# GLA and NSA attention in one block of 44 slots, with the eight sample items at every fourth slot from the tenth

## The reference, cut to what matters

```
x = LN1(a*x + 0.5*FFN1(x))
(gq, gk, gv, ga, gr, nq, kc, vc, ks, vs, kw, vw, ng) = split(x @ w_in)
log_a = log_sigmoid(ga @ w_gate2 + b) / 16
o_g, S = gla_chunked(gq, gk, gv, log_a, S0)            # 4 heads, dk 128, dv 256
o_g = head_rms_norm(o_g) * silu(gr)
q, kc, ks, kw = rope(...)                              # 16 query heads, 4 kv heads, hd 64
k_cmp, v_cmp = gelu(blocks(kc|vc) @ w1) @ w2           # 15 compressed rows per sequence
o_n = g0*cmp_attention + g1*sel_attention + g2*window_attention
x = LN2(a*x + [o_g | o_n] @ w_out)
x = LN3(a*x + 0.5*FFN2(x))
```

## Time and profile before

| | us |
|---|---|
| median of 3 runs | 2891.38 (2885.6 to 2896.63) |
| the profiled execution | 2894.41 |
| its span, first to last instruction | 2892.6 |
| TensorE busy | 2787.4 (96%) |
| DVE, ACT, POOL busy | 1579.8, 469.2, 789.0 |
| mean granted TensorE clock | 0.938 |

### The profile page before, as it was taken

The page is one execution under the profiler, slowest core; times in us unless marked ns, Lnnn a source line. Parts: engine busy times, 40 slices in busy tenths (PEclk is TensorE's granted clock), DMA queues, the critical chain, the costliest instruction groups (busy, mean ns, idle before and its releaser), DMA issues. The chain is left out here.

```text
span 2892.6 us, 45504 instructions
## 1 busy us (share of the span) xinstructions
PE 2787.4 (96%) x17763; PEld 2657.3 (92%) x17763; DVE 1579.8 (55%) x1547; ACT 469.2 (16%) x1098; POOL 789.0 (27%) x578
## 2 busy tenths in 40 slices
PE   8999999999999999999898998979999999999997
PEld 7999999899999889997686777969999999999996
DVE  5555555455555565543647435565565565555555
ACT  2110001111000220001424542041100000000002
POOL 1332332132234520000424002533213322322353
PEclk9999999999999999999656777979999999999998
DMA  6555555455555535663221214435465455555542
GB/s 185 153 150 156 149 145 155 123 153 149 156 150 144 133 104 151 145 148 106 92 88 32 59 38 116 116 102 145 135 169 146 132 158 159 142 140 161 153 130 82
DMA packets 735289, 379.76 MB, mean 131 GB/s; under 512 B 65515, under 2 KB 729963, under 8 KB 735163
## 3 DMA queue, kind: packets, MB, share of 16 engines
q1 hardware_dynamic: 735098, 378.93, 48.0%
q10 hardware_dynamic: 128, 0.05, 0.0%
HBM read 369.62 MB, written 13.38 MB: 132 GB/s over the span
## 5 line engine op out<-in xcount | busy, mean ns | idle before, releaser
L318 PE MATMUL bank<-xh_before,wh_before 128*128 128x320 f32 x2112 | 657.6, 311 | 13.8 <-DVE wl_before L336 13.7
L320 PE MATMUL bank<-xh_before,wl_before 128*128 128x320 f32 x2112 | 656.0, 311 | 0.0
L319 PE MATMUL bank<-xl_before,wh_before 128*128 128x320 f32 x2112 | 655.9, 311 | 0.0
L318 PE MATMUL bank<-xh_after,wh_after 128*128 128x320 f32 x1664 | 521.4, 313 | 22.0 <-DVE wl_after L336 13.4
L334 DVE CAST wh_before<-raw 128x2048 fp32r<-128x2048 f32 (+1 forms) x196 | 219.8, 1121 | 579.8 <-PE bank L320 537.3
L319 PE MATMUL bank<-xl_after,wh_after 128*128 128x320 f32 x1664 | 518.4, 312 | 0.0
L320 PE MATMUL bank<-xh_after,wl_after 128*128 128x320 f32 x1664 | 518.3, 311 | 0.0
L336 DVE TENSOR_TENSOR wl_before<-raw,wh_before 128x2048 fp32r<-128x2048 f32 (+1 forms) x196 | 463.3, 2364 | 6.7
L334 DVE CAST wh_after<-raw 128x2048 fp32r<-128x2048 f32 (+1 forms) x168 | 184.8, 1100 | 435.8 <-PE bank L320 435.6
L318 PEld LDWEIGHTS bank<-xh_before,wh_before 128*128 128x128 f32 x2112 | 399.5, 189 | 15.5 <-issue 12.1
L336 DVE TENSOR_TENSOR wl_after<-raw,wh_after 128x2048 fp32r<-128x2048 f32 (+1 forms) x168 | 409.4, 2437 | 5.8
(11 more groups left out here) (232 smaller groups left out, 3419.2 us busy)
## 6 DMA issues: line engine op xcount, KB each, us to landing
raw<-in_w_ffn_in SPq DMA_DIRECT2D x176, 1024.0 KB, 5.8
raw<-in_w_ffn_out SPq DMA_DIRECT2D x128, 704.0 KB, 4.8
raw<-in_w_in SPq DMA_DIRECT2D x36, 1024.0 KB, 5.6
raw<-in_w_in SPq DMA_DIRECT2D x16, 512.0 KB, 5.3
raw<-in_w_out SPq DMA_DIRECT2D x16, 512.0 KB, 4.3
raw<-in_w_out SPq DMA_DIRECT2D x64, 128.0 KB, 3.8
proj<-in_cache_cmp_kv SPq DMA_DIRECT2D x64, 64.0 KB, 2.4
raw<-in_state_gla SPq DMA_DIRECT2D x8, 512.0 KB, 4.6
```

Source lines behind the costliest of these rows:

```text
L318: pe.matmul(out, L.wh[a][:, w], hi[:, k], start=(k == 0), stop=False)
L319: pe.matmul(out, L.wh[a][:, w], lo[:, k], start=False, stop=False)
L320: last = pe.matmul(out, L.wl[a][:, w], hi[:, k], start=False, stop=(k == nk - 1))
```

## The change

`gla` and `attention` become one function with one block, `mixing_stage`. What it does:

- A start does what the first `gla` block and the start of `attention` did, in another order: six tiles (the keys) are rotated first, with DVE doing both of their products; then DVE makes the decay and the first two differences, and only then are the other eight tiles rotated. POOL makes the level-0 keys in the midst of its part of those eight. Token turns lie between the rotations, six of them after the compression. The compressed rows come last.
- Then 44 slots run. In slot i each engine does its part of attention as before, and after it `gla_step(i)`: step 0 the key turn and level 0, odd steps up to 15 a level, even steps up to 16 a sample's state, steps 17 to 20 two outputs each, step 21 the last state, steps 22 and 23 the mean squares, later steps the norm.
- GLA has two PSUM banks (6 and 7) in turn for all its products; attention keeps the others, so that the compressed scores have one bank instead of two, and turned keys and probabilities share one.
- Sample items stand at slots 9, 13, ... 37. Their keys are turned in halves over two slots. Their three small products with new and compressed rows become one, of 48 rows.
- The differences are made for half of each group with the right sign, so the absolute value on ACT is gone, and level keys and queries are scaled on one half of the columns.
- The causal mask is added in place to the last 128 columns of the scores only, and the maximum is read from PSUM.
- The space comes from the residual `xT`: it is stored to memory during the projection (2.62 MB) and loaded back at slot 24.

The diff, cut to what the prediction speaks of:

```diff
@@ projection, SyncE
                 segment(seg_a, 8, 0, 1)
+                sp.wait_ge(L.ln["kept"], before.t0 + KD)
+                sp.dma_start(L.x_kept, L.xT[:]).then_inc(L.x_out, 16)
                 segment(seg_r, 4, 8)
-def gla(L, s):
+def mixing_stage(L, s):
...
+    B, QL, KL, att = (L.xT[:, 4 * i:4 * i + 4] for i in range(4))
+    roped = [T_KV + i for i in (0, 1, 4, 5, 8, 9)] + [T_NQ + i for i in range(8)]
+    NR, NK = len(roped), 6
...
-    FIRST, EVERY = 17, 3
+    FIRST, EVERY = 9, 4
...
+    gjobs = [("turn", t) for t in range(3)] + [("score", 0, j) for j in range(3)]
+    for step in range(1, 2 * LEVELS + 1):
+        if step % 2:
+            gjobs += [("score", (step + 1) // 2, j) for j in range(parts((step + 1) // 2))]
+        else:
+            gjobs += [("inter", step // 2 - 1), ("state", step // 2 - 1, 0), ("state", step // 2 - 1, 1)]
+    O_STEP = 2 * LEVELS + 1
+    P_STEP, MS_STEP = O_STEP + 4, O_STEP + 5
...
+    def gbank(job):
+        return bank[6 + gjob_no[job] % 2]
@@ tensor
+            def claim(job):
+                j = gjob_no[job]
+                if j >= 2:
+                    pe.wait_ge(g_free[j % 2], j // 2)
+                return gbank(job), g_made[j % 2]
...
             def scores(i):
                 if i >= 2:
-                    pe.wait_ge(masked, 2 * (i - 1))
-                main, small = bank[i % 2], bank[2 + i % 2]
+                    pe.wait_ge(exped, 3 * (i - 1))
+                main, small = bank[i % 2], bank[2]
...
+                    if i:
+                        pe.wait_ge(masked, 2 * i)
                     pe.matmul(small[:, 32:48], qT, k_cmp[r, NB, p], start=True, stop=True).then_inc(scored, 1)
...
-                    for n in range(3):
-                        mm = pe.matmul(o, v_small[:, n, b, p * P:(p + 1) * P], pt[0:16, 4 + n, q],
-                                       start=False, stop=(n == 2))
+                    mm = pe.matmul(o, v_small[:, b, p * P:(p + 1) * P], pt[0:48, 4, at], start=False, stop=True)
...
+            for i in range(NR):
+                rotate(i)
+                if i >= 2:
+                    turn_tokens(i - 2)
+            pe.wait_ge(by_sin, NR)
+            for n in (1, 0):
+                compress(n)
+            for i in range(EARLY, NJ):
+                turn_tokens(i)
+            compressed_rows()
+            pe.wait_ge(biased, GH)
+            for i in range(SLOTS):
+                for n in range(2):
+                    if i + 2 - n in seq:
+                        turn_keys(seq[i + 2 - n], n)
                 if i < NI:
                     scores(i)
                 if LAG <= i < NI + LAG:
                     turn(i - LAG)
                 if i > LAG:
                     outputs(i - LAG - 1)
+                gla_step(i)
@@ vector
+            def gla_step(g):
+                if g < O_STEP and g % 2 == 0:
+                    lv = g // 2
+                    if lv + 2 <= LAST:
+                        difference(lv + 2)
+                    if lv < LAST:
+                        q_level(lv + 1)
+                    if g:
+                        state(lv - 1)
+                    else:
+                        merge(0)
+                elif g < O_STEP:
+                    merge((g + 1) // 2)
...
+            for i in range(NK, NR):
+                rope(i)
...
+            for i in range(SLOTS):
+                if i <= NI:
+                    item(i)
+                gla_step(i)
@@ gpsimd
+            for i in range(NK, NR):
+                pool.wait_ge(rope_done, i - 1)
+                pool.tensor_tensor(xc[:, i % 2], proj[:, roped[i]], L.cst[:, K_COS:K_COS + T], ALU.mult
+                                   ).then_inc(by_cos_pool, 1)
+                if i == NK + 3:
+                    k_level(0)
@@ scalar
+            for i in range(9):
+                take_tokens(i)
+            decay(0)
+            act.activation(EB[:], B[:, :, TP:T], ACT.Exp).then_inc(chain_a, 1)
+            decay(1)
+            for i in range(9, EARLY):
+                take_tokens(i)
...
+            act.activation(gr, gr, ACT.Silu).then_inc(acted, 1)
+            for i in range(EARLY, NJ):
+                take_tokens(i)
+            for i in range(SLOTS):
...
+                if LAG <= i < NI + LAG:
+                    take(i - LAG)
+                if i > LAG:
+                    out(i - LAG - 1)
                 if i < NI:
                     exps(i)
+                gla_step(i)
@@ sync
+                if i == MS_STEP + 2:
+                    for h in range(2, GH):
+                        await_made(sp, ("ms", h))
+                    sp.dma_start(L.xT[:], L.x_kept).then_inc(L.x_back, 16)
```

More of the change, by code:

```diff
@@ L186, in build @@
             L.cmp_w2 = sb("cmp_w2", [P, 2, HD], scope=mixing)
[L187 to L191, removed]
+            mixing_stage(L, mixing)
         open_operands(L, "after")
@@ L824, in settle @@
         self.eng.wait_ge(self.sem, self.n)
-def gla(L, s):
+def mixing_stage(L, s):
     nc, A, O, bank, proj = L.nc, L.A, L.O, L.bank, L.proj
     NS = NB * TS
[L832 to L845, removed]
+    ident = L.cst[:, K_ID:K_ID + P]
     q = proj[:, T_GQ:T_GQ + GH]
@@ L1271, in attention @@
-def attention(L, s):
-    nc, A, O, bank, proj = L.nc, L.A, L.O, L.bank, L.proj
-    mix = proj[:, T_NQ:T_NQ + 8]
-    ident = L.cst[:, K_ID:K_ID + P]
-    LAG = 3
+    inter = L.sb("inter", [P, 2 * GH, NS], scope=s)
+    s0 = [L.raw[i][:, 1024:2048].rearrange("p (h v) -> p h v", h=GH) for i in range(2)]
+    o_var, o_t = ([proj[:, at + h] for h in range(GH)] for at in (T_GQ, T_GK))
+    o_r = [proj[:, T_KV + 6 + 4 * (h // 2) + h % 2] for h in range(GH)]
+    LAG, NV = 3, 2
     RING = LAG + 1
-    S = [L.sb(f"scores{i}", [P, 2, GW], scope=s) for i in range(2)]
+    NEW, WIN, CMP = PAST, GW, 2 * GW
@@ new lines, in mixing_stage @@
+    g_made = [L.sem(f"gla_bank_made{i}") for i in range(2)]
+    g_free = [L.sem(f"gla_bank_free{i}") for i in range(2)]
+    state_in = [L.sem(f"state_in{i}") for i in range(2)]
+    state_out = [L.sem(f"state_out{i}") for i in range(2)]
+    rotated, by_cos, by_cos_pool, by_sin, rope_done = (L.sem("rope_" + x) for x in ("rotated", "cos", "cos_pool", "sin", "done"))
+    tokens, tokens_out, kv_stored = L.sem("tokens"), L.sem("tokens_out"), L.sem("kv_stored")
+    w1_in, w2_in, paired_k, paired_v, hidden, acted = (
+        L.sem("cmp_" + x) for x in ("w1_in", "w2_in", "paired_k", "paired_v", "hidden", "acted"))
@@ new lines, in _ @@
+                if i - LAG - 2 in seq and seq[i - LAG - 2] + NV < NB:
+                    b = seq[i - LAG - 2] + NV
+                    sp.wait_ge(out_ready, at_item[b - NV] + 1)
+                    past(b, 1, past_v[b % NV], v_in[b % NV])
+                if i == P_STEP + 1:
+                    for n in range(2):
+                        await_freed(sp, ("final", n))
+                    sp.dma_start(O["gla_p"][0, 0].rearrange("h k v -> k h v"), s0[0]).then_inc(L.stored, 16)
+                    L.n_stored += 1
@@ new lines, in turn_tokens @@
+            def turn_tokens(i):
+                what, t, n = tjobs[i]
+                if i >= 4:
+                    pe.wait_ge(tokens_out, i - 3)
+                rows = P if t < 2 else T - TP
+                to = bank[2 + i % 4]
+                if what == "g":
+                    mm = pe.transpose(to[0:rows, 0:48], L.gate[0:48, t * P:t * P + rows], ident[0:48, 0:48])
+                else:
+                    if what == "kv":
+                        pe.wait_ge(rope_done, NK)
+                    base = (T_GV if what == "v" else T_KV) + 4 * n
+                    for j in range(4):
+                        mm = pe.transpose(to[0:rows, j * P:(j + 1) * P], proj[:, base + j, t * P:t * P + rows], ident)
+                mm.then_inc(tokens, 1)
@@ L1424, in outputs, with turn_keys @@
-            def outputs(i):
-                pe.wait_ge(taken, 2 * turn_no[i] + 2)
+            def turn_keys(b, n):
+                if turn_no["k", b, n]:
+                    pe.wait_ge(taken, turn_no["k", b, n])
+                pe.wait_ge(k_in[b % 2], 64 * (b // 2 + 1))
+                for p in range(2):
+                    for g in range(NPG):
+                        mm = pe.transpose(bank[3][:, p * PAST + g * P:p * PAST + (g + 1) * P],
+                                          past_k[b % 2][:, n, g, p * P:(p + 1) * P], ident)
+                mm.then_inc(turned, 1)
@@ L1427, in outputs, with turn @@
+            def turn(i):
+                if turn_no["p", i, 0]:
+                    pe.wait_ge(taken, turn_no["p", i, 0])
+                pe.wait_ge(weighed, i + 1)
                 if i >= 2:
                     pe.wait_ge(out_taken, i - 1)
-                pt = PT[i % 2]
-                o_bank = bank[6 + i % 2]
+                w, x = PR[:, i % RING], bank[4 + i % 2]
+                chunks = min(width(i), PAST) // P
+                for n in range(2):
+                    at = WIN + 16 if n and i in seq else n * WIN
```

(74 more changed lines are left out.)

1005 lines of the change are left out of this document (472 added, 533 removed).

## The result

The changed kernel takes 2825.85 us (median of 4 runs, 2823.38 to 2827.64) against 2890.43 for the kernel before (4 runs): a ratio of 0.9775, 95% interval 0.9754 to 0.9796. The direction was right, the size was not.

A forecast was written before the change was run, and what follows sets the result against it. TensorE's own work divided by its granted clock was taken as the bound. Slots -31 us and start +10 gave -21, so 2891.4 - 20.5 = 2871 us, own range 2850 to 2890, overall range 2830 to 2907.

The forecast's parts named there:

- Slots 0 to 16: GLA's levels and states mixed with attention: 175 us of half-clock work at an assumed clock of 0.54, 162 us.
- the stage's forecast of 382: The whole mixing stage between input and output projection: slots 311 us and start 71 us.
- the prediction's own sign of being wrong: In the slots: the clock of either part differs by 0.08 or more from the forecast.
- Slots 17 to 43: Remaining attention and GLA work: 200 us at clock 0.85 and the last 17 at 0.51, 134 us.
- Waits: TensorE's idle time in the slots: 15 us kept of 17.8 before; new waits from shared banks taken at nothing.
- The start: From the projection's end to slot 0: 71 us, 10 more than before, bounds -3 to +18.
- the stall: In the start, POOL makes level-0 keys before the last four rotations' cosines: 5 us estimated, 0 to 8.
- the chain: In the start, DVE's decay chain, 6.4 us, and two differences, 3.0, go ahead of the compression.
- The residual's store: Storing 2.62 MB during the projection: 13 us of traffic, hidden, so 0; without cover up to +13.
- R2: Rival, much faster: denser mixture holds full clock longer, 0.65 and 0.95 in the slots, 2831 us; chance 0.14.
- R1: Rival, slower: clock does not rise, 2912 us; chance 0.18. Clock 0.72 or less in slots 17 to 40 eats the gain.
- R3: Rival, no change: DVE sets the pace, TensorE waits 0.7 us in each of 28 slots, 2891 us; chance 0.18.

The follow-up runs named there:

- e4_wide: The changed kernel with each state step's eight products of 8 moving columns widened to the 64 of all samples: 2806.37 us.
- e8_separate_wide: e1_separate with the state's narrow products widened to 64 columns as in e4_wide: 2833.49 us.
- e1_separate: The changed kernel with attention's slots starting 17 slots later than GLA's steps, so levels and states run without attention beside them: 2858.86 us.
- e3_long_values: The changed kernel with four more products of 16 rows in each sample's values, writing columns that nothing reads: 2861.19 us.
- e7_all: e5_wide_rows plus, in the start, DVE's decay chain behind all fourteen ropes and POOL's level-0 keys behind the last cosine: 2784.26 us.
- e5_wide_rows: e4_wide with the four wide products of each state step taking 128 rows instead of 64, the added rows zero: 2797.66 us.

## Why the prediction was wrong, step by step

- **Slots 0 to 16: the step that failed.** "So I take 0.54: 175 / 1.08 = 162 us." The work was about right: 122.6 busy us at 0.72 are 177 at the half clock by the prediction's own division. The clock was not, and that is 39.4 of the 51.6 us by which the stage's forecast of 382 missed. The reason given for 0.54 was half right: the state's 8-column products do hold the clock down (e4_wide, e8_separate_wide). What the prediction did not price is that attention's products in the same slots raise it again; it took a value between the parents' clocks (0.60 and 0.53), as if a mixture could not run faster than its parts. e1_separate shows that it does: the same work takes 25.3 busy us more when the two are apart. That sum is over both parts of the slots; how much of it lies in slots 0 to 16 the run does not separate. A clock of 0.72 against 0.54 is also the prediction's own sign of being wrong.
- **Slots 17 to 43.** 134 us forecast, 127.3 busy. Two errors met: the clock was 0.93 instead of 0.85 and 0.51, and the work at full clock is more than half of the half-clock price (6.02 and 3.28 for one item), which the division by the clock overlooked. Here the errors partly cancelled. Samples' values take 2.8 us at full clock, near the 2.6 forecast, and the falls behind them got rare, as the prediction said. e3_long_values prices what the prediction booked as length only, 8 x 2.2 us at the half clock: of the 35 us that it measured, 20 went when the same products had 128 rows.
- **Waits.** 15 forecast, 3.1 + 5.8 = 8.9 measured. The shared banks cost little.
- **The start.** 71 forecast, 71.63 measured, with the stall in its place. TensorE idles 9.3 and 4.5 us where the prediction had 9.4 for the chain and 5 for the stall. But the compression took 13.9 us where it had 11.8, and what lies behind it 11.8 where it had 13.8, so the total is in part luck. That the chain could lie mostly beside the compression was not seen.
- **The residual's store.** TensorE is busy 299.36 of 300 us in the projection, 299.48 before, with DMA at 0.60 instead of 0.58: hidden, as said.
- **Rivals.** R2 was nearest (2831), at 0.65 and 0.95, and its reason, that the denser mixture holds the clock longer, is what e1_separate shows; the prediction gave it 0.14. Even it had slots 0 to 16 too slow. R1's point of decision, 0.72 in the later slots, was not reached: 0.93. R3's waits on DVE are 1.0 us.

Left open: what the spacing of the samples alone is worth, what the rows alone are worth, and why the later slots of e4_wide and e7_all hold 0.89 where e5_wide_rows holds 0.96; a fall at 1564 in e7_all comes behind the same ACT waits of 1.14 and 0.72 us, but that wait was not taken away. Why thin products go with a lower clock no run shows; the runs show only that they do.

## What to carry to other kernels

Where TensorE is busy throughout and its granted clock lies low, ask which products fill little of the array, and widen or pad them with data that is there: eight times the columns cost 0.05 us in sixteen of these instructions and gave 19.5 us in all. Price a mixture of two stages by a run or by bounds, not by the mean of its parents' clocks. A chain of another engine that stands ahead of work ready for TensorE belongs beside TensorE's longest stretch that doesn't need it. Profile a kernel more than once before a clock of one stretch carries an argument.

## What the runs showed of the hardware that was not expected

- Sixteen matmul instructions with 8 moving columns took 1.95 us at the full clock, with 64 columns 2.00.
- GLA alone with 8 columns ran at 0.63 with TensorE busy 97%, with 64 columns at 0.94 with TensorE busy 89%.
- Padding with zeros went with a higher clock: with 64 added rows of zeros in the state's wide products slots 0 to 16 ran at 0.95 to 1.00 in three kernels, without them at 0.90 in one profile.
- 32 products of 16 rows, 10 to 11 us of length, cost 35 us; with 128 rows 15 us.
- The same 64 instructions of the compression took 13.9 us at 0.50 and 7.4 us at 1.00.
